# Time mix of a hybrid decoder step on one Trainium2 core: where the next head pair's decay and rate products, its first Strassen product and one VectorE sum stand in the written order

## The reference, cut to what matters

```
r, wl, k, v, al = token-shifted slices of the input projection
w = -softplus(-(w0 + tanh(wl) @ w_decay2)) - 0.5
decay = exp(-exp(w))
a = sigmoid(a0 + al @ w_a2)
kk = k * k_k / |k * k_k|
k = k * (1 + (a - 1) * k_a)
S_t = S_{t-1} * decay_t - (S_{t-1} kk_t) (kk_t * a_t)^T + v_t k_t^T
o_t = S_t r_t
```

## Time and profile before

| | us |
|---|---|
| median of 3 runs | 1483.86 |
| lowest, highest | 1481.19, 1487.07 |
| the profiled execution's own time | 1483.12 |
| its span, first to last instruction | 1481.5 |
| PE busy | 1448.7 (98%) |
| DVE busy | 858.0 (58%) |
| ACT busy | 555.9 (38%) |
| POOL busy | 370.8 (25%) |
| granted TensorE clock, mean of the span | 0.992 |

### The profile page before, as it was taken

How to read it: one execution, slowest core, us unless ns; L and a number is a source line. 1 busy time by engine, 2 the same in 40 slices (tenths; PEclk the granted TensorE clock), 3 DMA queues, 4 the chain that set the end, 5 groups by cost and what they waited for, 6 DMA issues and landing times.

```text
span 1481.5 us, 36383 instructions
## 1 busy us (share of the span) xinstructions
PE 1448.7 (98%) x14518; PEld 1078.5 (73%) x14518; DVE 858.0 (58%) x1730; ACT 555.9 (38%) x1356; POOL 370.8 (25%) x482
## 2 busy tenths in 40 slices
PE   7999999999999999999999999999999999999998
PEld 4555577777888888777777777777777777777753
DVE  3154566668777777474858676767676522023533
ACT  3166555541222222256363535454545232210000
POOL 0000141220111111125132221213131046355452
PEclk9999999999999999999999999999999999999999
DMA  9813698833466664421121212111112225342311
GB/s 328 319 57 110 169 263 286 248 99 111 125 161 163 157 157 128 118 56 39 36 55 32 54 33 53 42 44 42 45 40 59 55 83 171 86 153 75 121 43 50
DMA packets 191519, 165.35 MB, mean 112 GB/s; under 512 B 38550, under 2 KB 169622, under 8 KB 190327
## 3 DMA queue, kind: packets, MB, share of 16 engines
q1 hardware_dynamic: 182343, 128.15, 30.9%
q0 software_dynamic: 8352, 32.52, 7.4%
q10 hardware_dynamic: 656, 2.36, 0.5%
HBM read 136.91 MB, written 26.08 MB: 110 GB/s over the span
## 4 chain that ended last, share of the span: by engine, by line
PE 88%; DVE 7%; DVEq 1%; ACT 1%; issue 1%; DMA 0%; SPq 0%; POOL 0%; ACTq 0%
PE me_bank L3275 13%; PE rw_bank L1915 11%; PE sa_psOs L1250 8%; PE sa_psS L1203 7%; PE pr_psZ L754 4%; PE me_bank L3313 3%; PE fr_bankL L317 3%; PE fr_bankL L251 2%; DVE rw_gram L2777 2%; PE rw_bank L1951 2%; PE pr_psS L742 2%; PE sa_psT L1213 2%; PE rw_bank L1927 2%; PE rw_bank L2010 1%; PE rw_bank L2029 1%; PE pr_psO L777 1%
## 5 line engine op out<-in xcount | busy, mean ns | idle before, releaser
L1915 PE MATMUL rw_bank<-hT,big 128*128 128x288 f32 x336 | 97.7, 436 | 0.0
L1311 ACT COPY kpe<-sa_psS 128x512 f32<-128x512 f32 x64 | 34.4, 589 | 134.0 <-PE sa_psS L1203 134.0
L1915 PEld LDWEIGHTS rw_bank<-hT,big 128*128 128x128 f32 x336 | 63.3, 199 | 17.7 <-ACT big L2424 1.7
L1040 POOL DMA_DIRECT2D big<-in_cache_kv x68 | 37.6, 553 | 145.8 <-issue 145.8
L754 PE MATMUL pr_psZ<-hT,qlT 128*128 128x288 f32 x256 | 73.9, 408 | 0.0
L3351 ACT COPY big<-me_bank 128x288 f32<-128x288 f32 x42 | 16.7, 398 | 144.8 <-PE me_bank L3275 144.8
L1040 POOL DMA_DIRECT2D pages<-in_cache_kv x68 | 37.5, 552 | 117.1 <-issue 117.1
L754 PEld LDWEIGHTS pr_psZ<-hT,qlT 128*128 128x128 f32 x256 | 46.6, 189 | 20.2 <-issue 8.5
L1250 PE MATMUL sa_psOs<-big,sa_ST 128*128 128x257 f32 x256 | 60.3, 385 | 0.0
L1250 PE MATMUL sa_psOs<-pages,sa_ST 128*128 128x257 f32 x256 | 60.3, 385 | 0.0
L1407 DVE TENSOR_TENSOR sa_ST<-sa_psT,kinvp 128x512 f32<-128x512 f32 x64 | 42.9, 679 | 23.6 <-PE sa_psT L1213 23.6
(11 more groups left out here) (653 smaller groups left out, 3702.7 us busy)
## 6 DMA issues: line engine op xcount, KB each, us to landing
big<-in_w_in SPq DMA_DIRECT2D x44, 512.0 KB, 3.9
big<-in_cache_kv POOLq DMA_DIRECT2D x68, 128.0 KB, 4.6
pages<-in_cache_kv POOLq DMA_DIRECT2D x68, 128.0 KB, 3.4
fr_wada<-in_w_ada SPq DMA_DIRECT2D x8, 1024.0 KB, 11.4
big<-in_cache_kv SPq DMA_DIRECT2D x60, 128.0 KB, 3.0
pages<-in_cache_kv SPq DMA_DIRECT2D x60, 128.0 KB, 3.1
qk_scratch<-oaT SPq DMA_DIRECT2D x32, 192.0 KB, 2.6
fr_wada<-in_w_ada SPq DMA_DIRECT2D x2, 2048.0 KB, 13.2
```

The lines of the kernel that those rows point to most:

```text
L1040: e.dma_start(M.pages[s % 2][q * QP:(q + 1) * QP, g, :, 0:KL], src).then_inc(landed, 16)
L1311: nc.scalar.copy(S.rearrange("q (c p j) -> q p c j", c=2 * GP, p=GP)[:, :, cs, :], got[:, :, cs, :]).then_inc(copied, 1)
L1915: last = mm(into, held, moving, start=(k == 0 and n in (1, 2, 7)), stop=(k == K4 - 1), skip_group_check=True)
```

## The change

In PE's list, for pairs 1 to 6, lora_part(p, 0) moves ahead of level_w(i, 0), lora_part(p, 1) ahead of level_x(i, 0), and multiply(p, KR, 1) is cut into two halves, steps 0 and 1 ahead of level_w(i, 1) and steps 2 and 3 behind it. At the last pair the gate steps move the same way: 3, 3, 4 and 3 steps in the four places where 4, 4 and 5 stood. Pair 0 keeps its order. In DVE's list add_value_partial(i, 21) moves from behind begin_inverse(i, 2) to behind begin_inverse(i, 0). ACT's, POOL's and SP's lists are unchanged, and no instruction is added or taken away.

```
-                if i == 0:
-                    lora_part(1, 0)
+                if more:
+                    lora_part(p, 0)
+                else:
+                    gate_parts(range(0, 3))
                 level_w(i, 0)
                 if more:
-                    lora_part(p, 0 if i else 1)
+                    lora_part(p, 1)
                 else:
-                    gate_parts(range(0, 4))
+                    gate_parts(range(3, 6))
                 level_x(i, 0)
-                if i == 0:
-                    multiply(1, KR, 1, range(0, 2))
-                elif more:
-                    lora_part(p, 1)
+                if more:
+                    multiply(p, KR, 1, range(0, 2))
                 else:
-                    gate_parts(range(4, 8))
+                    gate_parts(range(6, 10))
                 level_w(i, 1)
                 if more:
-                    multiply(p, KR, 1, range(0 if i else 2, K4))
+                    multiply(p, KR, 1, range(2, K4))
                 else:
-                    gate_parts(range(8, 13))
+                    gate_parts(range(10, 13))
                 level_x(i, 1)
...
                     begin_inverse(i, 0)
+                    add_value_partial(i, 21)
                     grams(i, range(6, NU))
                     begin_inverse(i, 1)
...
                 begin_inverse(i, 2)
                 if i:
-                    add_value_partial(i, 21)
                     variance(i - 1)
                 level(i, 0)
```

More of the change, by code:

```diff
@@ L2234, in _ @@
                     token_major(i, c)
-                if i == 0:
-                    lora_part(1, 0)
+                if more:
+                    lora_part(p, 0)
+                else:
+                    gate_parts(range(0, 3))
                 level_w(i, 0)
                 if more:
-                    lora_part(p, 0 if i else 1)
-                else:
-                    gate_parts(range(0, 4))
-                level_x(i, 0)
-                if i == 0:
-                    multiply(1, KR, 1, range(0, 2))
-                elif more:
                     lora_part(p, 1)
                 else:
-                    gate_parts(range(4, 8))
+                    gate_parts(range(3, 6))
+                level_x(i, 0)
+                if more:
+                    multiply(p, KR, 1, range(0, 2))
+                else:
+                    gate_parts(range(6, 10))
                 level_w(i, 1)
                 if more:
-                    multiply(p, KR, 1, range(0 if i else 2, K4))
+                    multiply(p, KR, 1, range(2, K4))
                 else:
-                    gate_parts(range(8, 13))
+                    gate_parts(range(10, 13))
                 level_x(i, 1)
```

## The result

| | before | after |
|---|---|---|
| median, us (12 runs each, same chip) | 1483.19 | 1489.07 |
| lowest, highest | 1478.38, 1487.07 | 1486.96, 1492.51 |
| ratio of after to before | | 1.0041, 95% interval 1.0028 to 1.0053 |
| profiled execution's own time | 1483.12 | 1486.96 |
| its span | 1481.5 | 1485.3 |

The change costs 5.9 us, 0.4%: a small loss, within the 0.5% that the prediction called no change, and 1 us from its 1488. The profiled execution of after is the fastest of its twelve. The engines do the same work as before; what changed is where PE stands idle. The first view is the stretches of after that answer to the earlier trace rows, PE alone: from lora part 0, which now opens the pair, to the start of level_x(i, 1), pairs 1 to 6; the seventh is the last pair, which answers to the earlier trace rows.

The account below looks back on a forecast made before the run. The prediction took PE to bound the kernel (88% of the chain of waits). 4.9 - 1.3 - 0.7 + 1.0 = +3.9 us on the profiled 1483.12 gave 1487.0, against the median 1488; range for 8 in 10: 1481 to 1495.

Parts of the forecast that it names:

- Lora part 1 ahead of level_x(i, 0): PE, pairs 1 to 6: part 1 keeps its time, level_x(i, 0) starts 1.70 us later; stretch +0.82 us per pair.
- The rival that part 1 does not wait for ACT: PE's opening, pairs 1 to 6: part 0 fills DVE's wait, nothing is given back; -15 us, 1469; chance 0.06.
- The rival that the opening is hidden anyway: PE's opening: nothing moves but the last pair, time within 2 us of before; chance 0.09.
- The sum on DVE: DVE's moved add_value_partial delays the last gram copies, which token_major waits for: 0.06 us, bounds 0 and 0.34.
- Next in line: PE's out_transposed waiting for DVE's level 1: 0 us taken, bounds -0.1 to +0.2.
- The holds: Unexplained holds of level_w in pairs 3 and 5, 1.36 us together: half taken as gone, -0.7 us.
- The last pair: PE's gate steps and small groups in the last pair: waits go, -1.3 us, bounds -1.4 and 0.
- The clock: PE's granted clock falls in 4 of 6 pairs instead of 3, at 2.1 us: +1.0, bounds -7.5 and +10.5.

Follow-up runs that it names:

- e1: After, with ACT's two sigmoids of lora part 0 moved ahead of the three W copies in pairs 1 to 6: 1476.18 us.
- g3: After, with lora part 1 and the whole of product 1 back in their old places in pairs 1 to 6: 1477.32 us.
- g1: After, with part 0's sigmoids ahead of the W copies, POOL's four first sums ahead of powers, and DVE's bonuses behind level(i, 1): 1472.69 us.
- f2: After, with two useless 128x128 by 288 products on PE ahead of lora part 1 in pairs 1 to 6: 1484.73 us.
- g2: Before, with one useless 128x128 by 288 product on PE ahead of level_w(i, 0) in pairs 1 to 6: 1479.31 us.
- e2: After, with ACT's sigmoids of part 0 ahead of gate_half but still behind the W copies: 1490.36 us.
- f4: After, with DVE's bonuses(i) behind level(i, 1) instead of ahead of it: 1489.16 us.
- f3: After, with product 1 in one piece behind level_w(i, 1) in pairs 1 to 6: 1498.24 us.
- e3: Before, with only DVE's add_value_partial(i, 21) moved as in the change: 1485.79 us.

## Why the prediction was right

*Lora part 1 ahead of level_x(i, 0)*, "the step that decides": right. It said that ACT's unchanged list would keep part 1 at its old time and push level_x(i, 0) 1.70 us back, with a stretch of 8.45 us. Measured: 1.42 us of wait, a little under the 1.5 to 1.8 foretold (in part because the profile gives the third group 0.31 us where I took 0.09), level_x 1.52 us later (4.51 against 2.99 us into the pair), a stretch of 8.50. The 0.82 per pair came out as 0.87. e1 and g3 confirm the cause from both sides.

*The rival that part 1 does not wait for ACT* said 1469. The trace of after refutes it, and e1 makes it true by moving the sigmoids: 1476.18. It was too optimistic because 0.54 us per pair comes back at POOL, a cover that I had named only for the change as it stood.

*The rival that the opening is hidden anyway* said no change within 2 us. The ratio's interval, 1.0028 to 1.0053, excludes no change, and the six pairs grew by 6.1 us.

*The sum on DVE*: 0.06 us was taken, 0.15 came; inside the bounds.

*Next in line*: 0 us was taken, 0.53 came, outside its bound of 0.2, though only in the two pairs at full clock. This term was mis-sized. I had moved DVE's operations by 1.70 us at their old durations and said that DVE and POOL would no longer meet in the same way. They meet worse: normalise took 1.89 in place of 1.08 us and gate_z 0.76 in place of 1.06, so the three operations took 0.51 us more than I moved them with. With 0.87 us six times and 0.53 twice, the term that I bounded by 4.3 and 6.1 us came to 6.3. The Trainium skill, "SBUF — State Buffer", section "Who interferes with whom", says that a DVE instruction with both inputs in the SBUF contends with a GpSimd instruction that reads it, through the port pair that they share. The two operations here are such a pair, both took longer where they met (normalise 0.81 and POOL's 0.46 us more), and the trace agrees. No run kept the two apart and changed nothing else, so that the port is the reason is not shown.

*The holds*: -0.7 was taken, -1.36 came; within bounds. e1, g1 and g3 have such holds again, of 0.2 to 0.8 us in other pairs, so nothing shows that the new order took them away; it may be an accident of this execution.

*The last pair*: -1.3 was taken, the stretch gave -1.23.

*The clock*: +1.0 was taken, with four falls at 2.1 us. Four pairs fell, and their price above 8.50 was 2.63 + 2.50 + 1.42 + 1.44 = 8.0 us against 7.5: +0.5. The reason that I gave was not sound in one point: I called 0.76 us the longest pause of PE before, but the earlier trace rows have one of 1.06 us in pair 3, which kept the clock. Nor is it shown that the thinner front is why four pairs fell and not three: pairs 3 and 4 of after have the same front, and only one of them lost the clock. f2 and g2 bear out that the clock's share hardly changed. The rule of the Trainium skill that I quoted ("TensorE: Matmul & The Clock Gate", Part 1) has the size right, 0.3% of the time on either side; but variants here differ by just that, and e2, f4 and f3 can't be ranked without it.

*The total*, +3.9 on the profiled execution, met +3.84, and that closely by luck: the two pieces that the change touches gave +6.1 and -1.3, and the 1.0 us that makes the difference lies before pair 1, where nothing was changed. The median, +5.9, does not hang on one such execution and lies in the range, 2 us above the sum. About half of these are the +0.5 us per full-clock pair at out_transposed.

Open: which pairs lose the clock in which execution. Only one trace of each kernel was read for it. The mean clock of the executions shows how much it varies: 0.987 to 0.996 for before, 0.984 to 0.994 for e2, about 1.1 us for each 0.001 among the executions of before. Why e2 and e3 had it lower is open, and what the holds are was not tried either.

## What to carry to other kernels

A piece of work that is moved forward in one engine's list starts no earlier than what it waits for on the others: read where its inputs stand in their lists, and move those first (here two sigmoids ahead of the W copies turned +6 us into -7). Otherwise the piece itself loses nothing, but everything queued behind it does. Then ask which wait is next: here it was POOL's sums, and behind them DVE's bonuses, each hiding a few tenths of a microsecond per pair. And when work of two engines slides against each other, its old durations no longer hold.

## What was unexpected of the hardware

**The clock falls without a long pause, and the same work does not always lose it.** In before the longest pause of PE in these stretches was about 1 us, and pair 6 lost the clock after 3.90 us in which PE counted as busy for 2.81, mostly in 32x32 products. Pairs 3, 4 and 5 did the same in their first 3.90 us, with the same busy time, and kept it. So it is in after: the first 3.83 us are alike in pair 3, which kept the clock, and in pair 4, which lost it 4.6 us after its start. The first row is pair 4 of before, the others pairs 3 and 4 of after, PE alone.

```profile
946.70:950.60 3.90, 2.82 (x149) 1.00 0.09 27
...
878.79:882.62 3.83, 1.91 (x78) 1.00 0.12 33
...
948.85:952.68 3.83, 1.91 (x78) 1.00 0.12 34
```

One useless 128x128 by 288 product of some 0.5 us per pair (g2) took the falls of the profiled execution from three to one, and two (f2) from four to none. Work that is no use paid for itself, 3 to 4 us in 1483. The busy share of PE in the opening alone does not tell whether the clock holds; what does is open.

**Two engines on one memory.** A 128x640 operation of DVE (normalise) took 0.81 us at best, 1.07 in before's pairs and 1.89 beside a 128x512 one of POOL, which itself went from 1.27 to 1.73.
